# FFN up products with 512 columns, over the high and the low input side by side, and a sum of squares by halving additions

## The reference

```python
def rmsnorm(x, g):
    y = xf * lax.rsqrt(jnp.mean(xf * xf, axis=-1, keepdims=True) + EPS)
    return (y * g).astype(x.dtype)

def conv_ffn(xn, up_w, conv_w, conv_b, down_w):
    h = causal_dwconv(xn @ up_w, conv_w, conv_b)
    g, u = h[..., :D_FF], h[..., D_FF:]
    return (jax.nn.silu(g) * u) @ down_w

def swiglu(h, w_gate_up, w_down):
    gu = h @ w_gate_up
    gate, up = gu[..., :D_FF_2], gu[..., D_FF_2:]
    return (jax.nn.silu(gate) * up) @ w_down
```

## Time and profile before

| | |
|---|---|
| median of 3 runs (lowest, highest) | 1969.28 us (1968.02, 1970.78) |
| the profiled execution, its span | 1973.29 us, 1971.6 us |
| granted TensorE clock, mean over the span | 0.971 of 2.4 GHz |
| TensorE, VectorE, ScalarE busy | 1888.6, 1298.1, 936.1 us |
| HBM read | 306.99 MB |

### The profile page before, as it was taken

How to read it: one execution, slowest core, us unless ns; L and a number is a source line. 1 busy time by engine, 2 the same in 40 slices (tenths; PEclk the granted TensorE clock), 3 DMA queues, 4 the chain that set the end, 5 groups by cost and what they waited for, 6 DMA issues and landing times.

```text
span 1971.6 us, 36438 instructions
## 1 busy us (share of the span) xinstructions
PE 1888.6 (96%) x14979; PEld 1831.3 (93%) x14979; DVE 1298.1 (66%) x1606; ACT 936.1 (47%) x1058; POOL 5.0 (0%) x31
## 2 busy tenths in 40 slices
PE   6988999999998899999999999999999999899998
PEld 6988899999985699999999999999999999799997
DVE  6968677777676487777556667555656556656555
ACT  5734455555453455555334445433534335544343
POOL 1000000000000000000000000000000000000000
PEclk9999999999995799999999999999999999899999
DMA  5633145565441145555554454555645554126551
GB/s 181 192 107 108 65 150 192 191 208 174 155 150 43 43 151 191 191 170 193 174 187 162 161 190 150 192 180 182 189 133 193 190 182 159 65 86 206 178 188 68
DMA packets 237639, 309.17 MB, mean 157 GB/s; under 512 B 8187, under 2 KB 213753, under 8 KB 237561
## 3 DMA queue, kind: packets, MB, share of 16 engines
q1 hardware_dynamic: 236520, 308.03, 47.5%
q10 hardware_dynamic: 1040, 0.03, 0.0%
HBM read 306.99 MB, written 1.05 MB: 156 GB/s over the span
## 4 chain that ended last, share of the span: by engine, by line
PE 60%; DVE 3%; ACT 1%; issue 1%; DVEq 0%; ACTq 0%
PE ps L566 13%; PE ps L568 13%; PE ps L567 13%; PE ps L592 6%; PE ps L595 6%; PE ps L594 6%; PE ps L818 1%; DVE weights_lo L1620 0%; PE ps L804 0%; ACT weights_hi L1056 0%; PE ps L789 0%; DVE residual L1673 0%; DVE normed_lo L1685 0%; DVE scratch L1691 0%; DVE scratch L2247 0%
## 5 line engine op out<-in xcount | busy, mean ns | idle before, releaser
L566 PE MATMUL ps<-normed_hi,weights_hi 128*128 128x256 f32 x3200 | 919.5, 287 | 16.5 <-DVE normed_lo L1685 11.1
L568 PE MATMUL ps<-normed_hi,weights_lo 128*128 128x256 f32 x3200 | 909.4, 284 | 0.0
L567 PE MATMUL ps<-normed_lo,weights_hi 128*128 128x256 f32 x3200 | 909.3, 284 | 0.0
L1620 DVE TENSOR_TENSOR weights_lo<-raw_weights,weights_hi 128x2048 fp32r<-128x2048 f32 x290 | 663.4, 2289 | 279.2 <-ACT weights_hi L1056 278.9
L1056 ACT ACTIVATE weights_hi<-raw_weights 128x2048 fp32r<-128x2048 f32 x290 | 551.6, 1904 | 300.9 <-PE ps L568 128.2
L566 PEld LDWEIGHTS ps<-normed_hi,weights_hi 128*128 128x128 f32 x3200 | 618.4, 193 | 22.1 <-issue 11.2
L567 PEld LDWEIGHTS ps<-normed_lo,weights_hi 128*128 128x128 f32 x3200 | 618.3, 193 | 3.2 <-issue 2.9
L568 PEld LDWEIGHTS ps<-normed_hi,weights_lo 128*128 128x128 f32 x3200 | 617.9, 193 | 0.0
L592 PE MATMUL ps<-down_in_hi,weights_hi 128*128 128x256 f32 x1440 | 410.1, 285 | 6.5 <-DVE down_in_lo L1705 3.4
L594 PE MATMUL ps<-down_in_lo,weights_hi 128*128 128x256 f32 x1440 | 409.1, 284 | 0.0
L595 PE MATMUL ps<-down_in_hi,weights_lo 128*128 128x256 f32 x1440 | 409.0, 284 | 0.0
(11 more groups left out here) (231 smaller groups left out, 1101.4 us busy)
## 6 DMA issues: line engine op xcount, KB each, us to landing
raw_weights<-in_ffn_w_gate_up_dram SPq DMA_DIRECT2D x88, 1024.0 KB, 5.1
raw_weights<-in_ffn_up_w_dram SPq DMA_DIRECT2D x44, 1024.0 KB, 5.1
raw_weights<-in_ffn_w_down_dram SPq DMA_DIRECT2D x44, 1024.0 KB, 4.9
raw_weights<-in_ffn_down_w_dram SPq DMA_DIRECT2D x22, 1024.0 KB, 4.9
raw_weights<-in_ssd_in_w_dram SPq DMA_DIRECT2D x20, 1024.0 KB, 5.4
raw_weights<-in_a_w_in_dram SPq DMA_DIRECT2D x14, 1024.0 KB, 5.1
raw_weights<-in_attn_in_w_dram SPq DMA_DIRECT2D x12, 1024.0 KB, 5.2
raw_weights<-in_ssd_out_w_dram SPq DMA_DIRECT2D x8, 1024.0 KB, 4.9
```

The source lines that it names most:

```text
L566: mm(o, hi, h_hi[:, k, :], start=(k == 0 and a == 0), stop=False, skip_group_check=True)
L567: mm(o, hi, h_lo[:, k, :], start=False, stop=False, skip_group_check=True)
L568: last = mm(o, lo, h_hi[:, k, :], start=False, stop=(k == DK - 1), skip_group_check=True)
L1620: tt(w_lo[:, s, :], raw[:, s, :], f32(w_hi[:, s, :]), ALU.subtract).then_inc(lo_split.sem, lo_split.plus())
```

## The change

The high and the low input move into one tensor `normed`, side by side for each chunk, so that one matmul with `weights_hi` takes 512 columns: the product with the high input lands in columns 0 to 255 of a PSUM bank, that with the low input in columns 256 to 511. The product of `weights_lo` with the high input (256 columns) is added into columns 0 to 255. Each of a unit's two output tiles thus has a bank of its own, and a unit two banks: gates use banks 4 and 5 (the second gate 0 and 1), ups banks 6 and 7. ScalarE copies the second halves into the scratch buffer `f_in` (`copy_low`), VectorE adds the first halves to it (`merge`) and then multiplies by `rstd` (`scale`), where one operation did it before. TensorE waits for the `evacuated` semaphore, set by `scale`, before it uses a pair of banks again, and once before the first down unit, whose banks the second gate had. The norm's sum uses bank 3 in an FFN. Only FFN up units change; other projections keep `up_unit`. In all norms and in the last one, the sum over the 8 chunks of squares is made by three additions of halves.

```diff
-        h_hi = sb("normed_hi", [P, DK, T], F32R)
-        h_lo = sb("normed_lo", [P, DK, T], F32R)
+        h = sb("normed", [P, DK, 2, T], F32R)
+        h_hi, h_lo = h[:, :, 0, :], h[:, :, 1, :]
...
-        STAT = 7
+        STAT, FFN_STAT = 7, 3
...
+            def wide_unit(b, first=False, ks=range(DK), reused=False):
+
+                s = slot[0]
+                if ks[0] == 0:
+                    pe.wait_ge(lo_split.sem, lo_split.next())
+                    if reused:
+                        pe.wait_ge(evacuated.sem, evacuated.value(-1))
+                    evacuated.n += 1
+                wh = w_hi[:, s, :].rearrange("p (k n) -> p k n", k=DK)
+                wl = w_lo[:, s, :].rearrange("p (k n) -> p k n", k=DK)
+                for k in ks:
+                    if first:
+                        pe.wait_ge(h_ready.sem, h_ready.next())
+                    for a in range(2):
+                        mm(ps[:, b + a, :], wh[:, k, a * P:(a + 1) * P], h[:, k, :, :].rearrange("p c t -> p (c t)"),
+                           start=(k == 0), stop=False, skip_group_check=True)
+                        last = mm(ps[:, b + a, 0:T], wl[:, k, a * P:(a + 1) * P], h_hi[:, k, :],
+                                  start=False, stop=(k == DK - 1), skip_group_check=True)
+                if ks[-1] == DK - 1:
+                    last.then_inc(su_done.sem, su_done.plus())
+                    slot[0] = (s + 1) % RING
...
             def ffn(stats=True):
-                up_unit(first=True)
+                wide_unit(4, first=True)
                 if stats:
-                    second_up()
+                    wide_unit(6, ks=range(DK // 2))
+                    norm_sum(b=FFN_STAT)
+                    wide_unit(6, ks=range(DK // 2, DK))
                 else:
-                    turn_small(FOX_HEADS)
-                    up_unit()
-                up_unit()
-                if stats:
-
-                    pe.wait_ge(evacuated.sem, evacuated.value(-2))
-                up_unit()
+                    turn_small(FOX_HEADS, FFN_STAT)
+                    wide_unit(6)
+                wide_unit(0)
+                wide_unit(6, reused=True)
+                pe.wait_ge(evacuated.sem, evacuated.value(-1))
                 down_unit(first=True)
                 with c.repeat(FU - 2, {lo_split: 3, evacuated: 2, su_done: 3, hid_ready: 1}):
-                    up_unit()
-                    up_unit()
+                    wide_unit(4, reused=True)
+                    wide_unit(6, reused=True)
                     down_unit()
...
+            def copy_low(w, b):
+                f(f_in[:, w, :, :], low_part(b), ACT.Copy).then_inc(low_copied.sem, low_copied.plus())
+
...
+            def merge(w, b):
+
+                dve.wait_ge(low_copied.sem, low_copied.next())
+                tt(f_in[:, w, :, :], main_part(b), f_in[:, w, :, :], ALU.add).then_inc(step.sem, step.plus())
+
+            def scale(w):
+                dve.wait_ge(step.sem, step.value())
+                tt(f_in[:, w, :, :], f_in[:, w, :, :], rows(rstd[:], 2),
+                   ALU.mult).then_inc(evacuated.sem, evacuated.plus())
...
+            def add_chunks(sq, total):
+
+                for half in (4, 2):
+                    tt(sq[:, 0:half, :], sq[:, 0:half, :], sq[:, half:2 * half, :],
+                       ALU.add).then_inc(step.sem, step.plus())
+                    dve.wait_ge(step.sem, step.value())
+                tt(total, sq[:, 0, :], sq[:, 1, :], ALU.add).then_inc(sums_ready.sem, sums_ready.plus())
...
-                    v.tensor_reduce(total, sq.rearrange("p k t -> p t k"), AX_X,
-                                    ALU.add).then_inc(sums_ready.sem, sums_ready.plus())
+                    add_chunks(sq, total)
...
                 if ahead:
                     dve.wait_ge(su_done.sem, su_done.next())
+                    merge(0, 4)
                     split_next()
...
                 def up(j, renew=True):
                     dve.wait_ge(su_done.sem, su_done.next())
-                    evacuate(f_in[:, 1, :, :], slot[0])
+                    merge(1, 6)
+                    scale(1)
...
+                trip(0, down_slot, 0)
                 u0 = unit[0]
-                with c.repeat(FU - 2, per_trip(**extra)) as i:
-                    trip(i, down_slot)
+                with c.repeat(FU - 3, per_trip(**extra)) as i:
+                    trip(i + 1, down_slot)
```

More of the change, by code:

```diff
@@ L1211, in ffn, with trip @@
                 give(down_slot)
-                extra = dict(evacuated=2, gate_act=1, hidden_ready=1, act_hi_made=1)
+                extra = dict(evacuated=2, gate_act=1, hidden_ready=1, act_hi_made=1, low_copied=2)
                 if conv is not None:
                     extra.update(conv_base=2, gate_ready=1)
-                def trip(j, s, last=False):
-                    gate(j + 1)
+                def trip(j, s, b=4, last=False):
+                    gate(j + 1, b)
                     up(j + 1, renew=not last)
@@ L1793, in trip @@
                         split_next()
+                trip(0, down_slot, 0)
                 u0 = unit[0]
-                with c.repeat(FU - 2, per_trip(**extra)) as i:
-                    trip(i, down_slot)
-                unit[0] = u0 + 3 * (FU - 2)
+                with c.repeat(FU - 3, per_trip(**extra)) as i:
+                    trip(i + 1, down_slot)
+                unit[0] = u0 + 3 * (FU - 3)
                 trip(FU - 2, last_slot, last=True)
```

46 lines of the change are left out of this document (28 added, 18 removed).

## The result

The change takes 1960.35 us (median of 5 runs, 1959.16 to 1961.61), the kernel before 1970.78 us on the same chip (5 runs, 1968.02 to 1973.25). The ratio is 0.9945, with a 95% interval of 0.9935 to 0.9956: 10.4 us faster. The forecast was 1951.6 with a range of 1934 to 1963. The direction and the range held, the gain was forecast at 17.7 us. The profiled execution took 1959.16 us with a span of 1957.0 and a mean granted clock of 0.973.

A forecast was written before the change was run, and what follows sets the result against it. TensorE's back-to-back matmuls bound the kernel, with VectorE close behind in convolutional FFNs. -26.8 + 10.9 - 0.5 - 1.25 = -17.7 us, from the profiled 1973.29 to 1955.6, from the median 1969.28 to 1951.6; range 1934 to 1963.

The forecast's parts named there:

- four plain FFNs: FFNs without a convolution: VectorE has slack, so the gain of the matmuls stays, 4 x 6.7 = -26.8 us.
- two convolutional FFNs: VectorE becomes the pace through the added merges, with idle time and half clock at the last down unit: +10.9 us together.
- sums: first plain stage, end of the kernel: Three additions replace the norm's reduction: -0.5 us in the first plain stage, -1.25 us at the kernel's end.
- the matmuls: FFN up units: a 512- and a 256-column matmul take 0.341 us a step instead of 0.360, gaining 0.019 us.
- Rival 4: Every matmul keeps 0.0133 us extra whatever its length: 4.7 us gained a stage, 1960 us; counted within the forecast's 67%.
- Rival 1: Extra paid by the column, so the new pair gains nothing: 1978.4 us, 9%; a neighbour saving only 0.003 us, 1974, 3%.
- the low part of the first down product: First convolutional FFN's start: VectorE finishes this split near 289.1 instead of 289.85, being reached a little sooner.
- the merge in the loop: VectorE's extra 512-element operation per up unit in the convolutional FFNs' loop: 0.81 us each, two in a trip.
- waiting about 0.5 us in each: Sign for convolutional trips of 17.2 us: TensorE waits about 0.5 us in each for the low split of the weights.

The follow-up runs named there:

- the last experiment: The kernel before, unchanged, executed once more for a second profile: 1970.66 us in that one execution.
- both ends narrow: The change, but the first two pairs and last pair of gate and up units in the convolutional FFNs use the old 256-column matmuls: 1952.62 us, ratio 0.9905.
- the last pair narrow: The change, but only the last pair of gate and up units in the convolutional FFNs uses the old 256-column matmuls: 1953.41 us, ratio 0.9908.

## Why the forecast was right, and where it was off

The stages of the profiled executions, forecast against measured:

| | forecast | measured |
|---|---|---|
| four plain FFNs | -26.8 | -11.6 (0.6 of it the first one's sum) |
| two convolutional FFNs | +10.9 | +7.8 |
| sums: first plain stage, end of the kernel | -1.75 | 0.6 (counted above) and -1.2 |
| the start and the parts between | 0 | -9.5 |

*That the range held is luck.* The terms that the forecast worked out come to -11.6 + 7.8 - 1.2 = -5.0 us; taken from its base of 1969.28 that is 1964.3, over the upper end of 1963. What brought the time to 1960.35 are stretches for which it had nothing.

*The step that failed* is in "the matmuls": "I take 0.2133 + 0.0078 = 0.221 for the long one". It is the size of one term: a long matmul takes 0.227 us by itself, 0.236 beside a short one, and the pair 0.353. Four plain stages gain 88 x 16 x 0.007 = 9.9 us by this, not 26.8. (Of the measured 11.6, some 1.5 in the third are clock: the kernel before runs its start at half clock in the first profile, 192.04 us, and not in the second, 190.55, and the change, 188.94, does not either.) Rival 4 had the long matmul right, 0.0133 us over its columns as for a short one. Its pair of 0.347 us, 4.7 us a stage, is still 0.006 short of the measured one (2.6 us a stage), by what only the alternation adds. Rival 1, no gain at all, was nearer to the truth than its 12% say: its threshold was 0.0065 us a step, measured were 0.007. The row misled: it belongs to another number format, 0.43 us for 512 columns where this one takes 0.227, and its small extra does not carry over.

The Trainium skill ("TensorE: Matmul & The Clock Gate", "Back-to-back issue gap") has a gap of N/2.4 + 2.5 ns, and calls it that of an isolated matmul; for a stream of loads and matmuls the section gives about 131 ns at 512 columns. By the rule a step gains 3 ns; the runs show 7. Neither figure holds for this format: 120, 173 and 227 ns stand where the rule says 109, 162.5 and 216. But that a step gains a few ns and not 19, as it has it, is what came out.

*The convolutional FFNs* went as forecast on VectorE's side: its slack gone; the first down unit 25.95 us after the stage's start (289.61 - 263.66; forecast 291.1 - 265.15 = 25.95); the last one with 3.2 us of waiting (3.7 in the second FFN, 4 forecast) and half clock behind it. The forecast's own figures for the low part of the first down product, 289.1, and for the trip that begins behind it, 289.67, do not agree; the start of 291.1 follows the second, and so did the run (288.14 - 263.66 = 24.48, against 24.52). Of VectorE's sizes the merge in the loop was off, 0.72 for 0.81. Eight trips of 17.03 for 17.19 are 1.3 us, and the last down unit came 190.29 us after the start and not 191.65. On TensorE's side the sign "waiting about 0.5 us in each" did not show, since its own trip is 17.1 us long and not 16.67; this is the step above once more. The drop of the clock behind the first wait was not forecast and costs nothing in the end: the two stages, one with it and one without, differ by 0.02 us.

*The sums* are right: -1.5 at a convolutional start, -0.6 and -1.2.

*The parts between.* By the stages the change is worth -11.6 + 7.8 - 1.2 = -5.0 us, and the runs give -10.4. The rest lies where the change does little, in what runs ahead of, between and behind the FFNs. Windows of the part with the differential attention, between the two convolutional FFNs, for the kernel before, its second profile, the change, and its second profile (the third number from the end is the clock):

```profile
458.85:691.53 232.68, 217.69 (x1382) 184.17 (x1381) 153.41 (x243) 109.37 (x163) 0.00 (x0) 0.86 0.34 112
```

```profile
458.86:691.67 232.81, 217.55 (x1383) 184.69 (x1381) 153.37 (x243) 109.39 (x163) 0.00 (x0) 0.86 0.34 112
```

```profile
461.25:689.40 228.15, 213.25 (x1382) 181.20 (x1381) 149.49 (x245) 108.60 (x162) 0.00 (x0) 0.88 0.34 112
```

```profile
459.78:690.62 230.84, 215.78 (x1383) 183.29 (x1382) 149.74 (x245) 108.90 (x162) 0.00 (x0) 0.87 0.34 111
```

The length follows the clock: 0.86, 0.86, 0.88 and 0.87 of full speed with 232.7, 232.8, 228.2 and 230.8 us. The share of the clock that is not granted, 0.14 of 232.7 and 0.12 of 228.2 us, is 33 and 27 us, which is the size of the difference. The additions alone leave it at 232.1 us, also at 0.86. The wide units alone have 228.1, the change with the old matmuls 227.9, and the wide units in the plain FFNs alone, whose convolutional stages are free of them, this:

```profile
457.04:684.80 227.76, 212.23 (x1382) 181.37 (x1381) 150.16 (x247) 109.35 (x163) 0.00 (x0) 0.89 0.35 114
```

Its second profile has 231.0 us, as the change's second has 230.8. In all profiles of kernels with the side-by-side input this part takes 226.6 to 231.0 us, in the three without it 232.1 to 232.8. So the shorter part goes with that code, not with the additions, nor with the long matmul, nor with wide units in the convolutional FFN ahead of it; and it varies by 3 us for one and the same kernel. The start of the kernel varies as well, 263.7 and 262.3 us in two profiles of the change against 265.2 and 265.1 before, and 265.2 in the first profile of the kernel for the plain FFNs.

In the second pair of profiles the spans differ by 1968.9 - 1958.7 = 10.2 us, of which about 6 lie in these parts. What the last experiment expected of them fails in half: the start and this part of the kernel before repeat within 0.2 us; the last part between FFNs does not (127.17 and 125.67), nor does the third plain stage (192.04 and 190.55). So in the differential attention the granted clock differs with the length, that much the windows show. Why the kernel before had the lower one both times, and whether a few us of other timing ahead of it decide that, no run here isolates; about 5 us of the 10.4 stay explained by place, not by cause. The same holds for the additions alone (-10.9 by the runs, some -5 by the stages).

## What to carry to other kernels

Before small operations are merged into long ones, the long one is best measured by itself, in a series at the end of the kernel: here a row of another number format stood in for it, and the gain came out at 0.007 us a step for 0.019. A change that lightens one engine and loads another belongs only where the other has slack; here one kind of stage had it and its neighbour, with the same code, did not, and the version for the plain FFNs alone is 13.6 us faster than the whole. Where an engine loses its slack, the price falls due at the ends of the stage, at the waits that the slack used to cover, and each of them can pull the clock down as well. A time inside the range is no proof of its working: here the worked-out terms came to half of the gain.

## What the runs showed of the hardware

- Float32r matmuls at 2.4 GHz start 0.120 us apart at 256 columns, 0.173 at 384 and 0.227 to 0.228 at 512 with weights of 128 columns, on an otherwise quiet core. The extra over 256, 384 and 512 cycles of 2.4 GHz is 13, 13 and 13 to 15 ns; with weights of 32 columns it is 7, 13 and 18.
- A pair of 512 and 256 columns takes 0.353 us, 6 ns more than the sum of the two cadences (0.227 + 0.120): 0.236 from the long one's start to the next, 0.117 from the short one's.
- Whether the clock falls behind a wait is not told by the wait's length alone in these traces. Behind waits of 3.0 and 3.2 us in the first convolutional FFN of the change it fell to half for 3.4 us each; behind 3.0 us in the second it did not, behind 3.7 us there it did. Behind 2.2 us it fell in the first stage with both ends narrow (193.66 us) and not in the second (192.47), and behind the 1.7 us of the first stage with the last pair narrow it did not.
